# Expert order found on chip by token counts, 64 slots for the four least loaded experts, a ring of nine weight slots

## The chip, the cores and the metric

One core of one Trainium2 chip runs the whole program in one launch. The metric is the device time in microseconds of one execution. Engines are named as in the profile: PE (TensorE matmul), PEld (its weight loads), DVE (VectorE), ACT (ScalarE), POOL (GpSimd), SP (SyncE, which here only issues DMAs and waits). A "q" behind an engine is its instruction queue: "SPq" rows are DMA issues.

## The reference, cut to what matters

Two layers on 256 tokens of 1024 features, all in float32. Layer 0 is dilated attention with a dense SwiGLU, layer 1 is a bidirectional RWKV-7 mixer with a mixture of eight experts, two for each token. The change is in the expert part:

```python
D_MODEL = 1024; SEQ = 256; N_EXPERTS = 8; TOP_K = 2; D_FF_EXPERT = 3584

def swiglu(h, w13, w2):
    gate, up = jnp.split(h @ w13, 2, axis=-1)
    return (jax.nn.silu(gate) * up) @ w2

def moe_swiglu(h, router, w13, w2):
    t = h.reshape(B * S, D)
    logits = (t @ router).astype(jnp.float32)
    top_val, top_idx = lax.top_k(logits, TOP_K)
    gate = jax.nn.softmax(top_val, axis=-1)
    combine = jnp.einsum('tk,tke->te', gate, jax.nn.one_hot(top_idx, N_EXPERTS, dtype=jnp.float32))
    out = jnp.zeros_like(t)
    for e in range(N_EXPERTS):
        out = out + combine[:, e:e + 1].astype(t.dtype) * swiglu(t, w13[e], w2[e])
    return out.reshape(B, S, D)
```

256 tokens with two experts each are 512 rows, 64 for an expert on average. For the inputs drawn with seed 0 the reference's router gives the eight experts 68, 57, 63, 68, 74, 65, 60 and 57 tokens.

## The kernel before, in words

The weights of one expert are 44 MB in 21 units of 2 MB (`U_EXPERT`): 14 "up" units (256 gate and 256 up columns each) and 7 "down" units. `expert_plan` (L129) gives their order: up 0 to 3, down 0, up 4, up 5, down 1, and so on, with downs 5 and 6 at the end. SP moves each unit as two DMAs of 1 MB (`halves`, issued at L597) into a ring of `R = 6` slots of 16 KB per partition. A slot is filled again when PE has used its unit: `wait_free_e` waits for `up_ps` or `down_ps`. Both up units of a pair count as used only after the pair's third run (below).

Experts run in the order 0 to 7, each with room for `CAP = 96` tokens. Tokens that don't fit would be computed in overflow passes after expert 7 (at most 5); each pass loads an expert's 21 units again.

PE's `expert` (L1559) computes for each pair of up units three runs of matmuls: for each unit one with 64 tokens as weights in each half of the array's columns (L1589), then one for both units with the 32 tokens 64 to 95, in four quarters (L1597). A down unit has a run for 64 tokens (L1564, `down_halves`) and one for 32 (L1571, `down_quarters`). ACT takes the SiLU (L2033), DVE multiplies (L2824) and turns the rows for the down product (L2805, L2815).

The router's results are worked on by DVE: ranks (L2724 and on), `choose` for expert 0, `addresses`, `two_rows` (the rows to which each token is copied), `shares` and `overflow_list` (L2749), in this order, and then its part of expert 0. POOL copies the tokens to `xg` in HBM with four indirect DMAs (L3081) once the rows are known. SP loads the tokens of expert n+1 into `xe` behind unit 10 of expert n (L765), and DVE turns them (`next_picked`, L2785). ACT stores each expert's result to `yd` in HBM. After expert 6 POOL gathers each token's rows of results from `yd` into `ya` (L3087), and DVE adds them during expert 7 (L2883). The last expert's result is scattered by PE (L1633, L1637), copied by ACT (L2060) and stored.

The ring's first expert units are issued at the end of the RWKV stage (`for u in range(BWO0, BWO0 + R)`): the two units of `bwo`, then a wait for `head_done` (the last head is normalized), then four expert units, then two more as `bwo`'s slots come free.

Of the kernel before, what the change touches and what calls it, by code (L numbers as in the profile page):

```python
# [6 lines left out]

# [8 lines left out]
F32 = mybir.dt.float32  # L16
I32 = mybir.dt.int32
# [5 lines left out]
P = 128  # L23
# [45 lines left out]
RING_SHIFT = tuple(len(range(r, U_QKV, RQ_SLOTS)) - U_QKV // R if r < RQ_SLOTS else -(U_QKV // R) for r in range(R))  # L69
GE = FFE // 256  # L70
CAP = 96
OVER = 5
# [9 lines left out]
C_ALL = C_CEN + 4 * P  # L82
# [3 lines left out]
def constants():  # L86
# [24 lines left out]
    for n, m in enumerate([(r <= q) - first, (r < q) - first, (r >= q) - last, (r > q) - last]):  # L111
        c[:, C_CEN + n * P:C_CEN + (n + 1) * P] = m
    return c, mask
# [27 lines left out]
def build(nc, x_in, xp_in, pos_in, const_in, mask_in, vec_in, rows_in, qk_rows, qk_cols, wqkv, awo, wrkv, w0, w1, w2, a0, a1, a2,  # L141
          g1, g2, bwo, fw13, fw2, router, mw13, mw2, out):
    ctx = ExitStack()
    with ctx:
# [86 lines left out]
        ones = m.take(P)  # L231
        full_e = m.take(4, 2 * EXPERTS)
# [10 lines left out]
        ya = m.take(2, T, D)  # L243
# [3 lines left out]
        base_e = m.take(EXPERTS)  # L247
# [6 lines left out]
        from_rows = m.take(2, T).bitcast(U32)  # L254

# [66 lines left out]
        E2Tm = [m.take(4, P) for _ in range(2)]  # L322
        Rp = [m.take(2, P) for _ in range(2)]
        m = Region(after_pads + 6 * KB * S, after_pads + 6 * KB * S + 5 * KB * LORA + KB * LORA)
        par_g, rowsB = [], []
        for _ in range(2):
            par_g.append(m.take(RQ))
            rowsB.append(m.take(2, RQ))
        z0e = [m.take(4, RH) for _ in range(2)]
# [16 lines left out]
        ar_late = [[lent.take(2, 2, P) for _ in range(2)] for _ in range(2)]  # L346
        bk = [lent.take(2, 2, P) for _ in range(4)]
        mo_early = [lent.take(4, P) for _ in range(2)]
        mo_first = [lent.take(4, P) for _ in range(2)]
        Xs = lent.take(16, P)  # L350
        lent = Region(5 * SLOT, R * SLOT)
        mo_late = [mo_first, [lent.take(4, P) for _ in range(2)]]
# [27 lines left out]
        slot_full = [sem(f"slot_full{i}") for i in range(R)]  # L380
# [14 lines left out]
        lg_ps, lg_sb, lg_ex = (sem(n) for n in ("lg_ps", "lg_sb", "lg_ex"))  # L395
        chosen_ok, place_ps, total_ps, over_ok = (sem(n) for n in ("chosen_ok", "place_ps", "total_ps", "over_ok"))
# [7 lines left out]
        gate_ps, gn_ms, gn_rt, db_ready = (sem(n) for n in ("gate_ps", "gn_ms", "gn_rt", "db_ready"))  # L404
# [31 lines left out]
        xg = nc.dram_tensor("xg", (EXPERTS * CAP + 2 * S, D), F32).ap()  # L436
        yd = nc.dram_tensor("yd", ((EXPERTS - 1) * CAP + 1, D), F32).ap()
# [85 lines left out]
        plans = [expert_plan(MOE0), expert_plan(MOE0 + U_EXPERT)]  # L523

        def arrived(eng, u, rounds=0):

            nth = u // RQ_SLOTS if u < U_QKV else u // R + RING_SHIFT[u % R]
            eng.wait_ge(slot_full[slot_of(u)], rounds * 32 + (nth + 1) * 32)

        def slot_of(u):  # L530

            return u % RQ_SLOTS if u < U_QKV else u % R
# [19 lines left out]
        free_e = {}  # L552
        for e in range(2):
            for kind, n, u in plans[e]:
                free_e[u] = (up_ps, e * UPS + 3 * (n // 2) + 3) if kind == "up" else (down_ps, e * GE // 2 + n + 1)
        per_turn = {up_ps: 2 * UPS, down_ps: GE}

        def wait_free_e(sp, u, i):

            w = u - R  # L560
            if w < MOE0 and isinstance(i, int) and i == 0:
                s, n = free[w]
                sp.wait_ge(s, n)
                return
            back = 0
            if w < MOE0:
                w, back = w + 2 * U_EXPERT, 1
            s, n = free_e[w]
            for t, per in per_turn.items():
                if s is t:  # L570
                    sp.wait_ge(s, i * per + (n - back * per))


        over_plan = expert_plan(U_QKV)
        over_uses = [len([v for v in range(U_EXPERT) if v % R == r]) for r in range(R)]
        uses = [len([u for u in range(MOE0 + EXPERTS * U_EXPERT) if u % R == r]) + RING_SHIFT[r] for r in range(R)]

# [15 lines left out]
        def _(sp):  # L593
# [80 lines left out]
            def rest_unit(u):  # L674
                if u < MOE0:
                    square(u, bwo[:, (u - BWO0) * 512:(u - BWO0 + 1) * 512])
                else:
                    expert_unit(plan_e[u - MOE0], 0)

            plan_e = [(e, *a) for e in range(2) for a in plans[e]]  # L680

            def expert_unit(item, i):

                e, kind, n, u = item
                tiled_unit(u, (mw13 if kind == "up" else mw2)[bass.ds(i * 2 + e, 1), n])
# [46 lines left out]
            key_rows(1)  # L732
            gate_params(0)
            gate_params(1)
            sp.wait_ge(za.ps, 2)
            lora_params(1)
# [17 lines left out]
            for u in range(BWO0, BWO0 + R):  # L754
                if u == BWO0 + U_BWO:
                    sp.wait_ge(head_done, NQ + 1)
                wait_free(u)
                rest_unit(u)

            def next_rows(item, i):  # L760

                e, at = item[0], plans[item[0]].index(item[1:])
                if at == 10 and not (isinstance(i, int) and i * 2 + e == EXPERTS - 1):
                    sp.wait_ge(picked_sb, (i * 2 + e + 1) * 2)
                    sp.dma_start(xe[0:CAP], xg[bass.ds((i * 2 + e + 1) * CAP, CAP), :]).then_inc(xe_in, 16)  # L765

            first = BWO0 + R - MOE0
            assert first < 10
            for item in plan_e[first:]:
                wait_free_e(sp, item[3], 0)  # L770
                expert_unit(item, 0)
                if item[3] == plans[0][9][2]:
                    sp.wait_ge(xg_in, 64)
                next_rows(item, 0)
            for i in range(1, EXPERTS // 2 - 1):
                for item in plan_e:
                    wait_free_e(sp, item[3], i)
                    expert_unit(item, i)
                    next_rows(item, i)
            for item in plan_e:  # L780
                wait_free_e(sp, item[3], EXPERTS // 2 - 1)
                expert_unit(item, EXPERTS // 2 - 1)
                next_rows(item, EXPERTS // 2 - 1)

            sp.wait_ge(over_ok, 1)
            many = sp.value_load(over_i[0:1, 0:1], min_val=0, max_val=OVER)
            with sp.Fori(0, OVER) as j:
                with sp.If(j < many):
# [4 lines left out]
                    for kind, n, u in over_plan:  # L793
                        if u >= U_QKV + R:
                            s, c = freed[u - U_QKV - R]
                            per = UPS if s is up_ps else GE // 2
                            sp.wait_ge(s, j * per + (EXPERTS * per + c))
                        tiled_unit(u, (mw13 if kind == "up" else mw2)[bass.ds(e, 1), n])
# [7 lines left out]
        def _(pe):  # L806
# [727 lines left out]
            run(ps[:, 6, 0:EXPERTS], [(ones, chosen[:, 0, :]), (ones, chosen[:, 1, :])]).then_inc(total_ps, 1)  # L1534
# [16 lines left out]
            def scatter(n, b, back, width):  # L1551

                pe.wait_ge(y_sb, n * 2 + 4)
# [5 lines left out]
            def expert(n, c, b, plan, landed, before_last=None):  # L1559
# [16 lines left out]
                for kind, g, u in plan:  # L1576
# [3 lines left out]
                    if kind == "up":  # L1580
                        w = unit(u).rearrange("p (k n) -> p k n", n=512)
                        p = g // 2
                        if p >= 2:
                            pe.wait_ge(hide_sb, n * UPS + (3 * (p - 2) + g % 2 + 1))
# [1543 lines left out]
```

## Time and profile before

| | |
|---|---|
| median of 3 runs | 1832.61 us (1832.45 to 1833.87) |
| span of the profiled execution | 1837.4 us |
| PE busy in it | 1787.1 us (97%) |
| DVE, ACT, POOL busy | 948.7, 349.1, 235.8 us |
| moved by DMA | 473.62 MB, of it 336 transfers of 1 MB from `mw`, the experts' weights |
| chain that ended last | PE 91%, DVE 5%, ACT 2%, DMA 1% |

The profiled execution took 4.8 us (0.3%) more than the median of the runs. In the page, part 2 cuts the span into 40 slices of 45.9 us, where each digit is a busy share in tenths; the experts fill the slices from the 21st on. A busy engine in this profile need not be the only limit: DMA engines and PE can both be full.

### The profile page before, as it was taken

To read this page: it belongs to the slowest core of one execution; us is meant where nothing else is said; L and a number is where in the kernel's file an instruction comes from. 1 tells how busy PE (TensorE), PEld (TensorE's weight loads), DVE (VectorE), ACT (ScalarE), POOL (GpSimd) and SP (SyncE) were. 2 spreads that over 40 slices of the span, in tenths; PEclk is the share of its full clock that TensorE was granted. 3 is DMA by queue.
4 is the path that set the end of the run, shared out by engine and by line. 5 is a ranking of instruction groups with operands and counts; after the bars stand their busy time and mean duration, and the time that the engine had idled before them with its cause. 6 is when DMAs were issued, how large, how long until landed. Compare 5 with 4: busy or idle time off the path is not lost.

```text
span 1837.4 us, 36427 instructions
## 1 busy us (share of the span) xinstructions
PE 1787.1 (97%) x15674; PEld 1173.0 (64%) x15674; DVE 948.7 (52%) x2350; ACT 349.1 (19%) x747; POOL 235.8 (13%) x319
## 2 busy tenths in 40 slices
PE   8999999999999998898999999999999999999998
PEld 5888885788445587887665555555555555555554
DVE  6667653655574567754364345354444544435442
ACT  3234332122012253352110000000000000000001
POOL 2432320100011434433000000000000000000000
PEclk9999999999999999999989999999999999999999
DMA  8552436744631011012479999999999999999994
GB/s 310 184 183 90 140 120 205 247 155 167 200 137 41 6 25 33 11 19 99 172 284 406 396 401 418 401 399 409 409 410 389 417 409 393 418 400 416 403 421 168
DMA packets 137958, 473.62 MB, mean 258 GB/s; under 512 B 30168, under 2 KB 59120, under 8 KB 94784
## 3 DMA queue, kind: packets, MB, share of 16 engines
q1 hardware_dynamic: 133904, 459.82, 64.9%
q0 software_dynamic: 2080, 7.37, 1.2%
q10 hardware_dynamic: 1808, 4.03, 0.6%
q8 instruction: 126, 2.06, 0.5%
q14 instruction: 40, 0.33, 0.1%
HBM read 461.09 MB, written 10.10 MB: 256 GB/s over the span
## 4 chain that ended last, share of the span: by engine, by line
PE 91%; DVE 5%; ACT 2%; DMA 1%; issue 1%; SPq 0%; POOL 0%; DVEq 0%
PE ps L1589 21%; PE ps L812 12%; PE ps L994 11%; PE ps L1597 11%; PE ps L1564 11%; PE ps L866 10%; PE ps L1571 5%; PE ps L1162 2%; PE ps L858 1%; PE ps L1008 1%; PE ps L1523 1%; PE ps L1509 1%; PE ps L886 1%; PE ps L820 1%; DVE arena L2530 1%
## 5 line engine op out<-in xcount | busy, mean ns | idle before, releaser
L1589 PE MATMUL ps<-arena 128*64 128x256 f32 x3584 | 397.1, 380 | 0.0
L1589 PEld LDWEIGHTS ps<-arena 128*64 128x64 f32 x3584 | 256.0, 137 | 150.3 <-issue 29.0
L812 PE MATMUL ps<-arena 128*128 128x128 f32 (+9 forms) x1946 | 279.5, 320 | 20.6 <-DVE arena L2518 9.1
L2824 DVE TENSOR_TENSOR arena<-arena,ps 64x256 f32<-64x256 f32 x168 | 71.3, 425 | 403.7 <-ACT arena L2033 403.6
L812 PEld LDWEIGHTS ps<-arena 128*128 128x128 f32 (+3 forms) x1946 | 222.2, 187 | 73.6 <-issue 39.3
L994 PE MATMUL ps<-arena 128*128 128x256 f32 x952 | 210.7, 379 | 0.1
L1597 PE MATMUL ps<-arena 128*32 128x256 f32 x3584 | 205.0, 381 | 0.0
L2033 ACT ACTIVATE arena<-ps 64x256 f32<-64x256 f32 x168 | 63.2, 376 | 738.9 <-PE ps L1589 554.3
L1564 PE MATMUL ps<-arena 128*64 128x512 f32 x896 | 203.1, 598 | 0.0
L994 PEld LDWEIGHTS ps<-arena 128*128 128x128 f32 x952 | 178.6, 190 | 23.8 <-issue 0.5
L866 PE MATMUL ps<-arena 128*128 128x256 f32 (+1 forms) x714 | 189.1, 425 | 0.0
L1597 PEld LDWEIGHTS ps<-arena 128*32 128x32 f32 x3584 | 111.0, 110 | 88.6 <-issue 21.5
L866 PEld LDWEIGHTS ps<-arena 128*128 128x128 f32 x714 | 134.8, 190 | 50.6 <-issue 34.4
L2805 DVE STREAM_TRANSPOSE arena<-arena 32x128 f32<-32x128 f32 x448 | 136.4, 304 | 7.3
L1564 PEld LDWEIGHTS ps<-arena 128*64 128x64 f32 x896 | 60.0, 136 | 119.9 <-issue 119.9
L2815 DVE STREAM_TRANSPOSE arena<-arena 32x64 f32<-32x64 f32 x448 | 106.5, 238 | 7.3
L1571 PE MATMUL ps<-arena 128*32 128x256 f32 x1792 | 107.2, 379 | 0.0
L3087 POOL DMA_INDIRECT arena<-yd,arena x4 | 3.8, 955 | 779.2 <-DMA yd<-arena 778.3
L2282 DVE TENSOR_TENSOR arena<-arena 128x1024 f32<-128x1024 f32 (+3 forms) x92 | 86.0, 959 | 22.0 <-PE ps L866 20.9
L1571 PEld LDWEIGHTS ps<-arena 128*32 128x32 f32 x1792 | 57.6, 110 | 43.4 <-issue 6.5
L1933 ACT ACTIVATE arena<-ps 128x512 f32<-128x512 f32 (+1 forms) x80 | 43.8, 560 | 49.5 <-PE ps L812 41.6
L2785 DVE STREAM_TRANSPOSE arena<-arena 32x128 f32<-32x128 f32 x168 | 50.9, 303 | 2.5
(304 smaller groups left out, 1440.0 us busy)
## 6 DMA issues: line engine op xcount, KB each, us to landing
arena<-mw SPq DMA_DIRECT2D x336, 1024.0 KB, 12.0
arena<-wqkv SPq DMA_DIRECT2D x35, 1024.0 KB, 7.3
arena<-fw SPq DMA_DIRECT2D x32, 1024.0 KB, 7.5
arena<-wrkv SPq DMA_DIRECT2D x12, 1024.0 KB, 7.3
arena<-awo SPq DMA_DIRECT2D x4, 1024.0 KB, 6.4
arena<-bwo SPq DMA_DIRECT2D x4, 1024.0 KB, 8.6
xg<-arena POOLq DMA_DIRECT2D x8, 384.0 KB, 9.0
arena<-xg SPq DMA_DIRECT2D x7, 384.0 KB, 17.1
```

Source lines behind the costliest of these rows:

```text
L812: last = mm(o, a, b, start=(n == 0), stop=(n == len(pairs) - 1))
L866: last = mm(ps[:, bank, 0:b.shape[2]], a[:, k, :], b[:, k, :], start=(start and k == 0), stop=(stop and k == n - 1), skip_group_check=True)
L994: last = mm(ps[:, bank, 0:256], a[:, k, :], b[:, k, :], start=(start and k == 0), stop=(stop and k == 3), skip_group_check=True)
L1564: last = mm(ps[r, 5, :], hidT[:, g % 2, k, 0:64], w[:, k, a * 512:(a + 1) * 512], start=(first and k == 0), stop=(end and k == 3), skip_gr ...
L1571: last = mm(ps[r, 6, 0:256], hidT[:, g % 2, k, 64:CAP], w[:, k, a * 256:(a + 1) * 256], start=(first and k == 0), stop=(end and k == 3), s ...
L1589: last = mm(ps[r, g % 4, 0:256], picked[:, b, k, 0:64], w[:, k, a * 256:(a + 1) * 256], start=(k == 0), stop=(k == KB - 1))
L1597: last = mm(ps[r, (7, 4)[p % 2], 0:256], picked[:, b, k, 64:CAP], pair[a % 2][:, k, a // 2 * 256:a // 2 * 256 + 256], start=(k == 0), stop ...
L2033: act.activation(sg_e[RH:P, j % 2, :], ps[0:RH, bank, 0:256], ACT.Silu).then_inc(sge_sb, 1)
L2282: dve.tensor_tensor(out, a, b, op).then_inc(sums_ok, 1)
L2805: dve.transpose(o[:, :, :, 32 * i:32 * i + 32], src[:, :, :, j, :])
L2815: last = dve.transpose(o[:, a, :, 64:CAP], src[:, :, j, :])
L2824: dve.tensor_tensor(hid_e[RH:P, p % 2, j % 3, :], sg_e[RH:P, j % 2, :], ps[RH:P, bank, 0:256], ALU.mult).then_inc(hide_sb, 1)
```

## The change

1. Order. From the token counts (PE's sums in `ps` bank 6) DVE's new function `turns` ranks the experts by count on chip, with expert 0 always first (`C_FORCE`), and gives turn n the rank `RANK_AT[n]` = 0, 4, 1, 5, 2, 6, 3, 7. Turns 1, 3, 5 and 7 thus take the four least loaded experts, if expert 0 is among the other four or not. SP reads each turn's expert number from `expert_no` and loads from that address. Places, weights and rows are put in turn order (`in_turn`). `turns` stands ahead of `addresses`; `overflow_list` moves from there to turn 1, behind DVE's pair 5 (`aside`).
2. Room. The light turns have `LIGHT = 64` slots and `per = 2` runs for each pair: the runs for tokens 64 to 95 (L1597, L1571) and their SiLU, product and turning are left out, each up unit's slot is free after its own run, and `xe`, `xg` and `yd` have 64 rows for them. Up to `OVER = 6` overflow passes.
3. Ring. Nine slots for the experts' units, in the order 3, 4, 5, 0, 6, 8, 1, 2, 7 (eight in the last turn: slot 8 is then `ya`). Small buffers of the RWKV stage move so that they fit. `first_free` lets the first nine units start as their slots' earlier use ends, the first right behind `bwo`; only the sixth still waits for `head_done`.
4. `gate_params(0)` and `(1)` are issued behind `lora_params(1)` and a wait for `rkv_ps` 8. Some semaphores are merged.

```diff
-OVER = 5
+OVER = 6
+LIGHT = 64
+RANK_AT = (0, 4, 1, 5, 2, 6, 3, 7)
+IS_LIGHT = tuple(r >= 4 for r in RANK_AT)
+ROOM = tuple(LIGHT if a else CAP for a in IS_LIGHT)
+RUNS_AT = tuple((2 if a else 3) * (GE // 2) for a in IS_LIGHT)
...
+        in_line = collections.deque((3, 4, 5, 0, 6, 8, 1, 2, 7))
+        for u in range(MOE0, MOE_END):
+            if u == MOE_END - U_EXPERT:
+                in_line.remove(8)
+            slot_in_turn.append(in_line[0])
+            in_line.rotate(-1)
...
-            gate_params(0)
-            gate_params(1)
             sp.wait_ge(za.ps, 2)
             lora_params(1)
+            sp.wait_ge(rkv_ps, 8)
+            gate_params(0)
+            gate_params(1)
             diagonal_blocks(0)
...
+            def first_free(u):
+                slot = slot_of(u)
+                if slot == 4:
+                    sp.wait_ge(E.ps, chain(NQ - 1, 1, 1))
+                elif slot in (5, 0, 6):
+                    sp.wait_ge(Y.ps, NQ)
+                elif slot == 8:
                     sp.wait_ge(head_done, NQ + 1)
+                elif slot in (1, 2):
+                    sp.wait_ge(*free[before_it[u]])
+                elif slot == 7:
+                    sp.wait_ge(lg_ps, T)
+            e = 0
+            for u in range(MOE0, MOE_END):
+                n, at = (u - MOE0) // U_EXPERT, (u - MOE0) % U_EXPERT
+                if n and at == 0:
+                    sp.wait_ge(order_ok, 1)
+                    e = sp.value_load(expert_no[0:1, n:n + 1], min_val=0, max_val=EXPERTS - 1)
+                if u < MOE0 + R + 3:
+                    first_free(u)
+                else:
+                    sp.wait_ge(*free[before_it[u]])
+                expert_unit(u, e)
+                if at == 10 and n + 1 < EXPERTS:
                     sp.wait_ge(xg_in, 64)
+                    sp.wait_ge(picked_sb, (n + 1) * 2)
+                    sp.dma_start(xe[0:ROOM[n + 1]], xg[ROWS0[n + 1]:ROWS0[n + 2], :]).then_inc(xe_in, 16)
...
+            def in_turn(dst, src):
+                n = src.shape[1]
+                link(dve.tensor_tensor(cmp_a[:, 0:n], turn_of.unsqueeze(1).broadcast_to([P, n, EXPERTS, EXPERTS]),
+                                       src.unsqueeze(2).broadcast_to([P, n, EXPERTS, EXPERTS]), ALU.mult))
+                link(dve.tensor_reduce(dst, cmp_a[:, 0:n], AX, ALU.add))
+            def turns():
+                E = EXPERTS
+                dve.wait_ge(place_ps, 2)
+                link(dve.tensor_copy(counts, ps[:, 6, 0:E]))
+                link(dve.tensor_tensor(keyed, counts, const[:, C_FORCE:C_FORCE + E], ALU.max))
+                other, own = keyed.unsqueeze(1).broadcast_to([P, E, E]), keyed.unsqueeze(2).broadcast_to([P, E, E])
+                link(dve.tensor_tensor(cmp_a[:, 0], other, own, ALU.is_gt))
+                link(dve.tensor_tensor(cmp_b[:, 0], other, own, ALU.is_equal))
+                link(dve.tensor_tensor(cmp_b[:, 0], cmp_b[:, 0], tie, ALU.mult))
+                link(dve.tensor_tensor(cmp_a[:, 0], cmp_a[:, 0], cmp_b[:, 0], ALU.add))
+                link(dve.tensor_reduce(rank, cmp_a[:, 0], AX, ALU.add))
+                link(dve.tensor_tensor(turn_of, ..., ALU.is_equal))
+                in_turn(expert_at[:, 0:1], const[:, C_ROW:C_ROW + E].unsqueeze(1))
+                dve.tensor_copy(expert_no, expert_at[:, 0]).then_inc(order_ok, 1)
+                in_turn(place2[:, :, 0:E], p8)
+                link(dve.tensor_copy(p8, place2[:, :, 0:E]))
+                in_turn(comb[:, :, 1:E + 1], logits)
+                link(dve.tensor_copy(comb[:, :, E + 1:2 * E + 1], comb[:, :, 1:E + 1]))
...
-                        if g % 2:
+                        if g % 2 and not light:
                             ...
                             for k in range(KB):
                                 for a, r in enumerate(QUADS):
                                     last = mm(ps[r, (7, 4)[p % 2], 0:256], picked[:, b, k, 64:CAP], ...)
...
+                        if light:
+                            down_halves(g, w, first, end).then_inc(down_ps, 1)
...
             picked_out(1, 0, CAP)
+            turns()
             addresses()
...
-            overflow_list()
...
+            for n in range(EXPERTS - 1):
+                expert(n, RUNS0[n], IS_LIGHT[n], n * 16 + 16, None, (n + 1) % 2, overflow_list if n == 1 else None)
```

## Rows read from the trace of the kernel before

**Rows 1.** The page, part 2: GB/s moved by DMA in 40 slices.

```profile
GB/s 310 184 183 90 140 120 205 247 155 167 200 137 41 6 25 33 11 19 99 172 284 406 396 401 418 401 399 409 409 410 389 417 409 393 418 400 416 403 421 168
```

**Rows 2.** Timeline of one period: start us, us, engine, line, count.

```profile
1201.05 7.08 PE L1589 MATMUL ps<-arena 128*64 128x256 f32 x64
...
1208.06 3.66 PE L1597 MATMUL ps<-arena 128*32 128x256 f32 x64
...
1211.54 1.91 PE L1571 MATMUL ps<-arena 128*32 128x256 f32 x32
...
1213.38 3.65 PE L1564 MATMUL ps<-arena 128*64 128x512 f32 x16
...
1216.86 7.08 PE L1589 MATMUL ps<-arena 128*64 128x256 f32 x64
```

**Rows 3.** SP's waits, 936 to 1811 us: total us, times, longest.

```profile
SPq L597 <- PE ps L1597: 534.0, 55, 26.0
```

**Rows 4.** DMA from 947.5 to 1810.5 us: busy tenths in 40 slices, total.

```profile
DMA  9999999999999999999999999999999999999998
...
DMA packets 49068, 349.33 MB, mean 405 GB/s; under 512 B 5504, under 2 KB 5504, under 8 KB 7503
```

**Rows 5.** Stretches: us, busy PE, PEld, DVE, ACT, POOL, clock, DMA share, GB/s.

```profile
932.00:947.50 15.50, 15.50 (x155) 11.23 (x154) 9.57 (x51) 0.96 (x3) 4.02 (x4) 0.86 0.25 99
...
1000.00:1100.00 100.00, 100.00 (x1132) 54.76 (x1132) 41.83 (x139) 8.34 (x21) 0.00 (x0) 1.00 1.00 400
...
1182.00:1212.00 30.00, 30.00 (x332) 16.57 (x332) 9.88 (x34) 2.10 (x6) 0.00 (x0) 1.00 0.99 375
1212.00:1260.00 48.00, 48.00 (x544) 26.41 (x540) 25.61 (x84) 3.55 (x10) 0.00 (x0) 1.00 1.01 419
```

**Rows 6.** DMA from 1800 to 1838 us in 40 slices of 0.95 us.

```profile
GB/s 423 423 431 431 397 414 345 190 43 52 0 0 0 0 0 0 0 0 0 0 0 17 0 0 0 0 0 9 0 0 9 17 0 177 367 272 276 30 9 0
```

**Rows 7.** The chain that ended last, its last pieces: start us, us, what.

```profile
1819.58 3.58 PE ps L1564 x16
1823.16 1.86 PE ps L1571 x32
1825.03 3.63 PE ps L1633 x8
```

**Rows 8.** Timeline of PE, POOL and DVE around the first expert's start.

```profile
936.83 7.13 PE L1589 MATMUL ps<-arena 128*64 128x256 f32 x64
...
941.76 1.11 POOL L3081 DMA_INDIRECT xg<-arena  x1 [16.20 <-DVE arena L2866]
...
944.72 0.23 DVE L2754 TENSOR_TENSOR arena<-arena 128x64 f32<-128x64 f32 x1
...
950.42 0.18 DVE L2765 CAST arena<-arena 128x11 int32<-128x11 f32 x1
...
954.43 2.00 DVE L2815 STREAM_TRANSPOSE arena<-arena 32x64 f32<-32x64 f32 x8
...
958.02 1.91 PE L1571 MATMUL ps<-arena 128*32 128x256 f32 x32
```

**Rows 9.** Timeline of SP's queue, 540 to 980 us.

```profile
573.68 0.49 SPq L700 DMA_DIRECT2D arena<-g  x1
...
623.41 3.77 SPq L710 DMA_DIRECT2D xd<-arena  x8
...
850.15 2.21 SPq L597 DMA_DIRECT2D arena<-bwo  x4
897.80 66.60 SPq L597 DMA_DIRECT2D arena<-mw  x22
```

**Rows 10.** Timeline of ACT: the copy behind the eighth `rkv_ps`.

```profile
608.82 0.60 ACT L1856 ACTIVATE arena<-ps 128x512 f32<-128x512 f32 x1 [6.53 <-PE ps L812]
```

**Rows 11.** Stretches ahead of a fall of the clock, columns as in rows 5.

```profile
840.80:847.60 6.80, 4.61 (x92) 3.72 (x90) 6.60 (x12) 0.54 (x2) 6.00 (x11) 1.00 0.09 25
847.60:851.00 3.40, 1.41 (x42) 1.14 (x37) 0.53 (x1) 0.61 (x2) 3.17 (x4) 1.00 0.32 34
```

More of the change, by code:

```diff
@@ L8 @@
+import collections
 import math
@@ L68 @@
 U_EXPERT = 21
-RING_SHIFT = tuple(len(range(r, U_QKV, RQ_SLOTS)) - U_QKV // R if r < RQ_SLOTS else -(U_QKV // R) for r in range(R))
 GE = FFE // 256
 CAP = 96
-OVER = 5
+OVER = 6
[4 more added lines that the diff above has]
+RUNS_AT = tuple((2 if a else 3) * (GE // 2) for a in IS_LIGHT)
+RUNS0 = tuple(sum(RUNS_AT[:n]) for n in range(EXPERTS + 1))
+RESULTS0 = tuple(2 + sum(1 if a else 2 for a in IS_LIGHT[:n]) for n in range(EXPERTS + 1))
+ROWS0 = tuple(sum(ROOM[:n]) for n in range(EXPERTS + 1))
+FULL = EXPERTS
 C_ID = 0
@@ L231, in build @@
         ones = m.take(P)
+        counts = m.take(EXPERTS)
+        keyed = m.take(EXPERTS)
+        rank = m.take(EXPERTS)
+        turn_of = m.take(EXPERTS, EXPERTS)
+        expert_at = m.take(2, EXPERTS)
+        expert_no = m.take(EXPERTS).bitcast(I32)
         full_e = m.take(4, 2 * EXPERTS)
@@ L328, in build @@
             rowsB.append(m.take(2, RQ))
+        m = Region(after_pads + 6 * KB * S, after_pads + 6 * KB * S + 5 * KB * LORA + KB * LORA)
+        assert m.at <= LATE_AT
+        E2Tm = [m.take(4, P) for _ in range(2)]
+        Rp = [m.take(2, P) for _ in range(2)]
         z0e = [m.take(4, RH) for _ in range(2)]
@@ L377, in mo_of @@
             return mo_late[q % 2][i // 2] if i % 2 else mo_early[i // 2]
-        slot_full = [sem(f"slot_full{i}") for i in range(R)]
+        slot_full = [sem(f"slot_full{i}") for i in range(R + 3)]
         in_x = [sem("in_x0"), sem("in_x1")]
@@ L548, in down_quarter @@
             return unit(DN0 + j)[:, 0:2 * h * D].rearrange("p (k n) -> p k n", n=D)[:, h * i:h * i + h, 512 * n:512 * n + 512]
[L552 to L576, printed above, removed]
+        for n, plan in enumerate(plans):
+            for kind, g, u in plan:
+                if kind == "down":
+                    free[u] = (down_ps, n * (GE // 2) + g + 1)
+                elif IS_LIGHT[n]:
+                    free[u] = (up_ps, RUNS0[n] + g + 1)
+                else:
+                    free[u] = (up_ps, RUNS0[n] + 3 * (g // 2) + 3)
+        over_plan = expert_plan(MOE_END)
+        over_uses = [slot_in_turn[MOE_END:].count(r) for r in range(R)]
         def x_scale(t):
@@ L672, in _, with expert_unit @@
                 square(RKV0 + n, wrkv[n // 2, :, (n % 2) * 512:(n % 2 + 1) * 512])
[L674 to L685, printed above, removed]
+            def expert_unit(u, e):
+                kind, g, _ = plans[(u - MOE0) // U_EXPERT][(u - MOE0) % U_EXPERT]
+                tiled_unit(u, (mw13 if kind == "up" else mw2)[bass.ds(e, 1), g])
             def tiled_unit(u, w):
@@ L1557, in scatter, with expert @@
                     run(ps[:, (4, 7, 0, 1)[k], :], [(pickT[0:width, b, t, :], yb[0:width, h * 512:(h + 1) * 512])]).then_inc(back_ps, 1)
-            def expert(n, c, b, plan, landed, before_last=None):
+            def expert(n, runs, results, light, c, b, plan, landed, before_last=None):
+                per = 2 if light else 3
                 def down_halves(g, w, first, end):
@@ L2782, in next_picked @@
                 rows = xe[:, 512 * half:512 * half + 512].rearrange("p (k j f) -> p k j f", j=4, f=32)
-                for i in range(CAP // 32):
+                for i in range(room // 32):
                     for j in range(4):
```

281 lines of the change are left out of this document (139 added, 142 removed).

## The prediction

> **What bounds the kernel now.** I read the slices of the page first. From the 22nd slice to the 39th DMA moves 389 to 421 GB/s and never rests; this is the expert stage, and nowhere else are two slices in a row above 300 [rows 1]. The change is about PE's work in this stage, so the question is which of PE and DMA sets its length. The timeline of PE shows a strict period of 1216.86 - 1201.05 = 15.81 us for each pair of up units and its down unit, without a wait: 7.01 us for the two runs of 64 tokens, 3.48 for the quarters with tokens 64 to 95, 1.84 for the down quarters and 3.48 for the down halves, each taken from start to start [rows 2]. Seven periods are 110.7 us for an expert and 885.4 for eight. SP waits 534 us for L1597 to free slots [rows 3], so PE sets the pace. But the view of DMA over the same stage shows that nothing is left there either: 349.33 MB in 863 us, 405 GB/s, with every slice but the last at nine tenths or more [rows 4]. The cleanest stretch, without a token load or a result store, has 419 GB/s at a DMA share of 1.01; a stretch with the load of `xe` has 375, and the first full 100 us have 400 [rows 5]. A PE period takes three units, 6.29 MB, so PE asks for 398 GB/s of weights alone. PE and DMA are full at once, and only what shortens both shortens the stage.
>
> **Part 1, PE's runs.** A light expert loses 3.48 + 1.84 = 5.32 us of 15.81 in each of seven periods [rows 2]: 37.2 us, and four of them 149 us. A light expert alone would then ask for 6.29 MB in 10.49 us, 600 GB/s. No row has this. A heavy and a light turn together are 110.7 + 73.4 = 184.1 us of PE, but 42 units, 88.1 MB, which at 405 GB/s take 217 us. Nine slots let PE run ahead for part of the first light turn; after that it waits for weights. I count these 149 us as nothing by themselves: PE will wait for DMA instead. The end is then set by the DMA stream: its start, its bytes, its rate, and the work behind its last unit.
>
> **Part 2, the start of the stream.** Before, four expert units are issued from 897.80 on, behind `head_done`, and two more when `bwo` frees its slots [rows 9]; then DMA falls to 99 GB/s between 932 and 947.5, a share of 0.25, since all six slots are full [rows 5]. The seventh unit starts when PE has freed the first pair: 936.83 + 10.49 + about 0.2 = 947.5 [rows 8, 2]. After, nine units fit. The first can be issued right behind `bwo` at 852 [rows 9], at a time when the page has 99 to 172 GB/s [rows 1], and all nine should land by about 938. PE's first turn is heavy in both kernels and needs the same runs, so the stream restarts at 947.5 again, but three units, 6.29 MB, are behind it already.
>
> **Part 3, the bytes of the stream.** 349.33 MB of before [rows 4], less 6.29 for the three units, less 0.52 for the four light loads of `xe` (128 KB less each), less 0.39 for three light stores of `yd`, plus 1.5 for the scatter to `xg`: in before it mostly ran in the idle 932 to 947.5 (99 GB/s for 15.5 us) and now it comes later (next part). That is 343.6 MB. At 405 GB/s it takes 848 us. The load of `xe` costs more than its bytes: 30 us at 375 instead of 419 lose 3.2 us for 0.39 MB, which alone would take 0.9 [rows 5]. Four loads that are a third smaller save about one us each instead of 0.3, so I take 845 us. Bounds: at 419 GB/s throughout 820 us, at the 400 of the slowest 100 us 859 [rows 5].
>
> **Part 4, DVE's `turns`.** About 17 small instructions. DVE's like ones between 944.72 and 950.42 follow each other at about 0.2 to 0.3 us [rows 8], so 17 x 0.27 = 4.6 us, between 2 (if it were only 0.12 each) and 8. It stands ahead of `addresses`; queued behind it on DVE are the row numbers, for which POOL's scatter waits, and the products of the first pair. `overflow_list`, 944.5 to 950.6, leaves this place, so DVE reaches its first expert about 1.5 us earlier than before. That matters as PE's first down at 958.02 has only 1.6 us over the end of DVE's turning at 956.43 [rows 8]. Cost nothing; should `turns` take 8 us, PE would lose 0.3. The scatter starts at 946.4 instead of 941.76, hence its bytes in the sum. SP waits for it ahead of the first `xe` load, now near 948; behind that wait is unit 11, whose slot is free only at 958, so nothing is late. `overflow_list` in turn 1, now some 46 instructions or 10 us, delays DVE's pair 6 there; PE could wait some 3 us for it in front of the last down, at a time when it is ahead of what DMA allows. Nothing. If DMA were no limit, 3 us.
>
> **Part 5, SP.** The address of a turn's expert comes from a register. SP waits for `order_ok` (about 941) at unit 21, which is issued near 1000, and nothing is late. Issues with a register address are not in the trace; a 1 MB issue takes SP some 0.43 us, and with six or more units queued in front of DMA even 2 us more would be hidden. A deeper queue is not in the trace of this stage either; I take no change and leave its risk to the range. The moved `gate_params` wait for the eighth `rkv_ps`, which ACT's copy shows at 608.82 [rows 10]. Behind the wait stands `diagonal_blocks(0)`, whose first DMA is at 623.41, so four issues of about 0.5 us fit in between [rows 9]. First use of the gates is after that. Nothing; without this cover it would cost these 2 us. The next `xe` lands behind unit 10, while PE still waits for units 11 and 12; DVE's block there has a period of DMA as cover.
>
> **Part 6, the end.** Before, the weights stop at about 1809.5 [rows 6], while PE starts the last unit only at 1819.58 [rows 7]: it is ten us behind the stream. After, PE stands at the end waiting for the last unit. Behind it come 3.58 us of halves (the 1.86 of quarters are gone), and then what lies between 1825.03 and the end of the span at 1837.4, 12.4 us [rows 7]: 16.0.
>
> **The sum.** 947.5 + 845 + 16.0 = 1808.5 us of span. The profiled span was 4.8 us above the median of the runs, so 1803.7; I say 1803. PE's own time would be 936.8 + 4 x 184.1 + 12.4 = 1685.6; the difference of 123 us should show as waits of PE for `mw`.
>
> [...]
>
> **Rivals.** (a) PE alone decides and DMA follows at any rate. For it: PE has no wait in the stage, and SP waits for PE. Against it: the DMA share of 1.00 at 400 to 419 GB/s. Time 1685.6 - 4.8 = 1681. Chance 0.03.
> (b) The stream is faster than its mean once the stage holds fewer loads, stores and PE reads: 420 GB/s or above, 818 us, and 947.5 + 818 + 16.0 - 4.8 = 1777. For it: the slices at 421 [rows 1]. Against: the dips come with token loads, which stay. Chance 0.12.
> (c) The clock, on the slower side. [...] Chance 0.05. [...]
> (d) A deeper queue or register addresses slow the stream to 390 GB/s: 881 us, 1840. No row has such a queue beside full-speed PE. Chance 0.10 for anything from 1818 up, about half of it below 1829.
> (e) The change doesn't save what it says, as an expert has more tokens than room: an overflow pass loads 44 MB more, 109 us, and about 20 us around it, 1932. The reference's counts give the heavy turns 68, 74, 68, 65 and the light turns 63, 60, 57, 57, all within room. Chance 0.02.
>
> **How the numbers follow.** The forecast, a stage bound by DMA at the rate of before, has 0.68 and its own range is 1786 to 1818 (the rates 400 to 415). About 0.2% is what a measurement of this kernel can tell from no change, so the same is 1829 to 1836. Faster: 0.68 + 0.03 + 0.12 + half of (d) = 0.88. Same 0.04. Slower 0.08: the rest of (d), (c) and (e). The range reaches from the 419 GB/s bound, 1779, up to 1824, half way into (d).
>
> **What would show each step.** Right: DMA share 1.0 and 400 to 419 GB/s from 947.5 to about 1793; no slice at 99 GB/s apart from the few us before 947.5; the first `mw` issue near 852; PE waiting some 120 us for DMA `mw`, nearly all in light turns; 64-token periods of 10.5 us where PE has weights; L1597 and L1571 with half of their counts; the first expert matmul within one us of 936.8; the last unit's run within 1 us of its landing. Wrong: PE waits well below 100 us with an early end would be (b) or (a); clock marks below 1.0 in light turns would be (c); mean rate below 400 with share 1.0 would be (d).

## The result and the profile after

The changed kernel takes 1803.76 us (median of 4 runs, 1802.29 to 1806.16) against 1832.6: a ratio of 0.9833, 95% interval 0.9815 to 0.9851, 28.8 us less. Forecast were 1803 and a range of 1779 to 1824.

The page of the changed kernel: span, part 2 with PE, clock, DMA and GB/s in 40 slices of 45.0 us, and the chain that ended last.

```profile
span 1800.6 us, 31353 instructions
...
PE   8999999999999998998999997999779996799877
...
PEclk9999999999999999999989999999999999999999
DMA  9452426754640000102759999999999999999995
GB/s 328 176 187 80 155 97 204 234 179 170 180 182 24 24 22 13 31 17 79 285 198 387 419 398 420 419 400 419 394 421 409 403 420 389 421 401 413 419 421 244
...
SPq L623 27%; PE ps L837 12%; PE ps L1019 11%; PE ps L891 10%; DMA arena<-mw 6%; PE ps L1616 6%; PE ps L1624 3%; PE ps L1591 3%; PE ps L1187 2%; PE ps L883 1%; PE ps L1598 1%; PE ps L1548 1%; PE ps L1534 1%; PE ps L1033 1%; PE ps L911 1%
```

PE now has sevens and sixes where it had nines, while DMA has nines as before and moves 387 to 421 GB/s, the level of [rows 1]. In the expert stage the chain no longer runs mainly through the experts' matmuls (before, L1589, L1597 and L1564 had 43% of the span) but through SP's issues (L623, 27%) and the landing of `mw` (6%). The three following views are of the stage alone. First, what PE waits for from 930 us on (in all, times, longest, us):

```profile
PE ps L1616 <- DMA arena<-mw: 64.2, 47, 2.7
PE ps L1591 <- DMA arena<-mw: 38.7, 25, 3.5
```

Second, DMA from 945 to 1782 us, busy tenths and total, the answer to [rows 4]:

```profile
DMA  8999999999999999999999999999999999999998
...
DMA packets 48078, 341.70 MB, mean 408 GB/s; under 512 B 5417, under 2 KB 5417, under 8 KB 7433
```

Third, the timeline of the first expert's start and the end of the chain, the answers to [rows 8] and [rows 7]:

```profile
929.63 7.13 PE L1616 MATMUL ps<-arena 128*64 128x256 f32 x64
...
940.40 2.05 SPq L623 DMA_DIRECT2D arena<-mw  x4
...
958.32 0.45 SPq L806 DMA_DIRECT2D arena<-xg  x1
```

```profile
1757.10 27.14 DMA arena<-mw
1784.24 0.04 issue
1784.28 3.65 PE ps L1591 x16
1787.94 3.63 PE ps L1660 x8
```

The stream restarts 10.8 us behind the first expert matmul and its last transfer lands at 1784.2, 843.8 us later. PE starts the last down unit 0.04 us behind it, where before it was ten us late [rows 6, 7].

The part ahead of the experts is of different length in different executions of the same code (last section), so the profiles are compared by the time from the first expert matmul to the end of the span, called the stage below. It is 1837.4 - 936.8 = 900.6 us before and 1800.6 - 929.6 = 871.0 after, 29.6 less, near the 28.8 of the medians. (A span is 1.7 us shorter than the time of the same execution: 1800.6 against 1802.29.)

### The profile page after: what moved, and what is told of

Read it like the earlier page. It is cut to its first block, busy times and chain, and to the rows that moved or that the text cites. A ratio compares the mean times of both kernels' runs of the same rounds, so it can differ in the third digit from the quotient of the medians.

```text
span 1800.6 us, 31353 instructions
## 1 busy us (share of the span) xinstructions
PE 1650.3 (92%) x12986; PEld 1082.1 (60%) x12986; DVE 873.5 (49%) x2082; ACT 339.2 (19%) x719; POOL 236.2 (13%) x319
## 4 chain that ended last, share of the span: by engine, by line
PE 56%; SPq 28%; DMA 7%; DVE 5%; ACT 2%; issue 2%; POOL 0%; DVEq 0%
SPq L623 27%; PE ps L837 12%; PE ps L1019 11%; PE ps L891 10%; DMA arena<-mw 6%; PE ps L1616 6%; PE ps L1624 3%; PE ps L1591 3%; PE ps L1187 2%; PE ps L883 1%; PE ps L1598 1%; PE ps L1548 1%; PE ps L1534 1%; PE ps L1033 1%; PE ps L911 1%
## 5 line engine op out<-in xcount | busy, mean ns | idle before, releaser
L1616 PE MATMUL ps<-arena 128*64 128x256 f32 x3584 | 405.2, 382 | 64.2 <-DMA arena<-mw 64.2
L2884 DVE TENSOR_TENSOR arena<-arena,ps 64x256 f32<-64x256 f32 x140 | 59.5, 426 | 473.5 <-ACT arena L2061 473.4
L1591 PE MATMUL ps<-arena 128*64 128x512 f32 x896 | 207.0, 606 | 38.7 <-DMA arena<-mw 38.7
L2061 ACT ACTIVATE arena<-ps 64x256 f32<-64x256 f32 x140 | 52.8, 377 | 723.0 <-PE ps L1616 631.0
L1591 PEld LDWEIGHTS ps<-arena 128*64 128x64 f32 x896 | 60.6, 138 | 162.4 <-issue 110.8
L2862 DVE STREAM_TRANSPOSE arena<-arena 32x128 f32<-32x128 f32 x448 | 136.3, 304 | 7.3
L1624 PE MATMUL ps<-arena 128*32 128x256 f32 x1792 | 102.5, 380 | 0.0
L1624 PEld LDWEIGHTS ps<-arena 128*32 128x32 f32 x1792 | 55.0, 110 | 44.8 <-issue 10.8
L2873 DVE STREAM_TRANSPOSE arena<-arena 32x64 f32<-32x64 f32 x224 | 53.3, 238 | 3.6
L1598 PE MATMUL ps<-arena 128*32 128x256 f32 x896 | 53.6, 379 | 0.0
L2842 DVE STREAM_TRANSPOSE arena<-arena 32x128 f32<-32x128 f32 x136 | 41.2, 303 | 5.1 <-DMA arena<-xg 3.0
L1598 PEld LDWEIGHTS ps<-arena 128*32 128x32 f32 x896 | 28.4, 110 | 22.1 <-issue 3.2
## 6 DMA issues: line engine op xcount, KB each, us to landing
arena<-mw SPq DMA_DIRECT2D x336, 1024.0 KB, 26.9
```

What stands on the lines that cost most here:

```text
L1591: last = mm(ps[r, 5, :], hidT[:, g % 2, k, 0:64], w[:, k, a * 512:(a + 1) * 512], start=(first and k == 0), stop=(end and k == 3), skip_gr ...
L1598: last = mm(ps[r, 6, 0:256], hidT[:, g % 2, k, 64:CAP], w[:, k, a * 256:(a + 1) * 256], start=(first and k == 0), stop=(end and k == 3), s ...
L1616: last = mm(ps[r, g % 4, 0:256], picked[:, b, k, 0:64], w[:, k, a * 256:(a + 1) * 256], start=(k == 0), stop=(k == KB - 1))
L1624: last = mm(ps[r, (7, 4)[p % 2], 0:256], picked[:, b, k, 64:CAP], pair[a % 2][:, k, a // 2 * 256:a // 2 * 256 + 256], start=(k == 0), stop ...
L2862: last = dve.transpose(o[:, :, :, 32 * i:32 * i + 32], src[:, :, :, j, :])
L2873: last = dve.transpose(o[:, a, :, 64:CAP], src[:, :, j, :])
```

## The experiments

All are edits of the changed kernel, unless named otherwise. Ratios are to the kernel before on the same chip. The experiments ran on four chips, where the kernel before has medians of 1834.2 to 1838.2 us against the 1832.6 of the result, so a difference between two ratios of up to some 0.003 (5 us) need not be the edit's. Where a step is that small, the stage in the profile decides, and it is one execution.

| run | edit | ratio (95%) | stage, us |
|---|---|---|---|
| changed | | 0.9833 (0.9815 to 0.9851) | 871.0 |
| e1 | all turns 96 slots | 0.9996 (0.9985 to 1.0008) | 902.1 |
| e2 | six ring slots | 0.9883 (0.9861 to 0.9904) | 884.0 |
| e3 | all turns 64 slots | 0.9753 (0.9734 to 0.9771) | 858.5 |
| e4 | a quarter fewer bytes | 0.9169 (0.9151 to 0.9188) | 751.0 |
| e5 | before, a quarter fewer bytes | 1.0005 (0.9995 to 1.0015) | 900.5 |
| e6 | first wait for the scatter later | 0.9812 (0.9799 to 0.9825) | 866.7 |
| e7 | no loads of `xe` | 0.9711 (0.9696 to 0.9726) | 848.8 |
| e8 | 96-slot turns first | 0.9787 (0.9769 to 0.9806) | 873.2 |
| e9 | `xe` loaded to 128 partitions | 0.9757 (0.9743 to 0.9771) | 857.2 |
| e10 | e6 and e9 | 0.9734 (0.9716 to 0.9752) | 854.7 |
| e11 | first units start as before | 0.9819 (0.9802 to 0.9836) | 870.1 |
| e12 | e10 and e8 | 0.9795 (0.9778 to 0.9812) | 863.7 |

**e1: everything but the light turns.**

```diff
-IS_LIGHT = tuple(r >= 4 for r in RANK_AT)
+IS_LIGHT = tuple(False for r in RANK_AT)
```

> The changed kernel, but every turn has 96 slots and three runs for each pair; order on chip, nine ring slots and the early start stay. Theory 'both full' (before, PE and DMA were both full; without fewer PE runs PE sets the stage again): eight heavy experts of 110.7 us behind the same first matmul, so 1832 us, ratio to before 0.998 to 1.001, and no waits of PE for mw. Rival 'ring' (the gain of 29 us comes from nine slots and the early start alone): 1804 to 1818 us.

Measured 0.9996. PE has no wait for `mw` and its period is the old one, as the timeline of PE shows:

```profile
1205.39 3.66 PE L1624 MATMUL ps<-arena 128*32 128x256 f32 x64
1208.87 1.91 PE L1598 MATMUL ps<-arena 128*32 128x256 f32 x32
1210.71 3.65 PE L1591 MATMUL ps<-arena 128*64 128x512 f32 x16
1214.19 6.00 PE L1616 MATMUL ps<-arena 128*64 128x256 f32 x54
```

Ring, early start, `turns` and the moved `gate_params` together neither gain nor cost anything that can be measured. Without fewer PE runs a faster stream is worth nothing.

**e2: the light turns without the ring.** `in_line` is (3, 4, 5, 0, 1, 2) and `first_free` waits for `head_done` at slot 3.

> The changed kernel with the light turns, but the ring has six slots in the old order and its first expert unit waits for the last head as before. Theory 'stream': the same bytes less nothing, and the three units that were behind the stream's restart come back into it, 6.29 MB at 405 GB/s = 15.5 us: 1819 us (1816 to 1824). Rival 'ring': all the gain goes, 1832 us. Rival 'PE': the light turns' runs alone carry the gain, so it stays at 1804 us.

Measured 0.9883, 0.005 or 9 us above the changed kernel, and 13.0 us in the profiled stage: the last unit lands 13.7 us later after the first expert matmul (868.3 instead of 854.6). "Stream" is confirmed, its 15.5 us a little too high. Of the 29 us 17 to 21 come with the light turns on six slots and 9 to 13 with the three more.

**e3: no 96-slot turn at all.** `IS_LIGHT` is all true, and the overflow list stays empty.

> The changed kernel with 64 slots and two runs in all eight turns and no overflow pass: tokens beyond an expert's 64th are left out. PE has 149 us less to do than in the changed kernel. Theory 'stream': the weights are the same bytes, only three loads of xe and four stores of yd are 128 KB smaller (0.9 MB, 2 to 4 us), so 1798 to 1803 us. Rival 'PE': 1655 us. If PE's work counts in part (the heavy turns, where both are full), something between, 1770 to 1790 us.

Measured 0.9753: PE has 149 us less to do and the kernel is 15 us faster (12.5 in the stage), so PE's work is not the limit. But I expected 2 to 4 us. The trace shows where the larger part comes from: in a light turn 0 PE frees the first slot after one run, and the stream restarts 4 us after the first matmul instead of 10.8. That is 7 of the 12.5, the smaller loads and stores 2 (0.9 MB). The other 3 to 4 us lie at the loads of `xe`: by the packets of the two traces, and against 420 GB/s, the last six loads lose 12.7 us of stream beyond their bytes here and 16.7 in the changed kernel. Why they lose less here was not followed.

**e4 and e5: a quarter fewer bytes, after and before.**

```diff
-                halves(u, (unit(u)[:, 0:half], unit(u)[:, half:]), (w[:, 0:half], w[:, half:]))
+                end = SLOT if u < MOE0 + 9 else SLOT - half // 2
+                halves(u, (unit(u)[:, 0:half], unit(u)[:, half:end]), (w[:, 0:half], w[:, half:end]))
```

> The changed kernel, but from the tenth expert unit on each unit's second half is loaded to one half only, so a unit moves 1.57 MB instead of 2.10; PE's work is unchanged (the rest of the slot holds old weights). The stream is 83 MB or 205 us shorter, less than PE's work. Theory 'stream': PE sets the stage, 4 x 184.1 us of it, 1681 us (1678 to 1690), and its waits for mw nearly vanish. Rival: if PE's waits come from SP's queue (register addresses, more waits) and not from the rate of DMA, they stay and the time is above 1740 us.

> The kernel before, with the same cut as in e4: from the tenth expert unit on a unit moves 1.57 MB instead of 2.10, PE's work unchanged. Theory 'both full': PE alone already set the pace before, with DMA just able to follow, so 1832 us on the first chip, ratio 0.998 to 1.001. Rival: if DMA had been the slower one there, each 1% of bytes would show, and the time falls by 20 us or more.

Measured 0.9169, 1680 us on the scale of the first chip, and 1.0005. With bytes to spare (371 GB/s at a DMA share of 0.94 in the first line below, columns as in [rows 5]) the changed kernel runs at the rate of its PE work, and PE waits 3.1 us in all from 950 to 1680:

```profile
1200.00:1300.00 100.00, 100.00 (x900) 54.67 (x897) 42.23 (x133) 8.35 (x21) 0.00 (x0) 1.00 0.94 371
...
PE ps L1592 <- DVE arena L2863: 3.1, 3, 2.8
```

The same cut brings nothing before. This pair carries the main reading: before, PE set the pace and DMA could just follow; after, DMA sets it, and 751.0 against 871.0 us of stage is what the light turns would be worth to PE alone.

**e6: SP's first wait for the scatter later.** From the trace of the changed kernel: SP issues units 9 and 10 at 940.4, then waits for the scatter to `xg` until 958.3, although PE has freed the slots of units 11 and 12 at 950.8. The windows of that time (us, busy of PE, PEld, DVE, ACT, POOL, clock, DMA share, GB/s) show DMA at rest for about half of 955 to 960:

```profile
945.00:955.00 10.00, 10.00 (x132) 5.23 (x129) 7.64 (x28) 0.75 (x2) 0.00 (x0) 1.00 1.00 413
955.00:960.00 5.00, 5.00 (x44) 2.83 (x40) 0.00 (x0) 0.18 (x1) 0.00 (x0) 1.00 0.46 167
960.00:966.00 6.00, 6.00 (x85) 3.54 (x84) 2.64 (x8) 0.57 (x2) 0.00 (x0) 1.00 1.01 390
```

```diff
-                if at == 10 and n + 1 < EXPERTS:
+                if at == (10 if n else 12) and n + 1 < EXPERTS:
```

> The changed kernel, with one edit: in turn 0 SP issues the first load of xe behind unit 12 instead of unit 10, so that units 11 and 12 do not stand behind SP's wait for the scatter (in the trace of the changed kernel that wait ends at 958.3, the slots of units 11 and 12 are free at 950.8, and DMA falls to 35 GB/s at 958 to 960). Theory 'stream': the stream is never interrupted again, 3.5 us less, 0.9814 of before. Rival: turn 0 is set by PE and the ring is refilled anyway, so the gap costs nothing and the ratio stays 0.9833.

Measured 0.9812, 0.0021 less, as "stream" wanted, but the intervals of the two ratios overlap, so the times don't settle it. The profiled stage is 4.3 us shorter and its last unit lands 3.7 us earlier after the first expert matmul, with the stream restarting 10.8 us behind that matmul in both. I take the gap as worth about 4 us, on this one pair of profiles.

**e7: the loads of `xe` taken out** (turns 1 to 7 compute on a constant).

> The changed kernel without the seven loads of xe (turns 1 to 7 compute on a constant instead of their tokens; SP's waits stay). Seven loads are 2.2 MB of 342. Theory 'bytes': 5.5 us less than the changed kernel, 0.980 of before. Theory 'slow packets' (while a load's 4 KB packets are in the queue, the weights' 8 KB packets take some 550 ns instead of 313, which loses about 2.5 us for each load beside its bytes): 20 to 24 us less, 0.970 to 0.972 of before.

Measured 0.9711, 22 us less than the changed kernel (22.2 in the stage): a load costs 3.2 us on average, while its 0.26 to 0.39 MB would be 0.6 to 0.9. "Slow packets" is right. A load in the changed kernel, in windows with the columns above:

```profile
1054.00:1066.00 12.00, 12.00 (x92) 6.50 (x90) 3.81 (x12) 1.13 (x3) 0.00 (x0) 1.00 1.02 423
1066.00:1072.00 6.00, 6.00 (x48) 3.26 (x46) 2.34 (x8) 0.08 (x1) 0.00 (x0) 1.00 1.03 259
```

The DMA share is full in both, the rate falls by two fifths. In the trace the weights' packets of 8 KB have a median of 313 ns in the first window and 506 ns in the second, where one in ten takes over 630. The stores of `yd`, from 96 or 64 partitions as well, do no such harm: they are still there in e7, and DMA keeps 417 to 423 GB/s in every slice of its stage but the first and the last.

**e9: the same loads to all 128 partitions.**

```diff
-                    sp.dma_start(xe[0:ROOM[n + 1]], xg[ROWS0[n + 1]:ROWS0[n + 2], :]).then_inc(xe_in, 16)
+                    sp.dma_start(xe[0:P], xg[ROWS0[n + 1]:ROWS0[n + 1] + P, :]).then_inc(xe_in, 16)
```

> The changed kernel, but each load of xe takes 128 rows to all 128 partitions instead of 96 or 64 (the rows beyond are not used; 1.4 MB more in all, 3.5 us at the stream's rate). Theory 'spread': the weights' packets slow down because a load to 96 or 64 partitions is laid out over the DMA engines in another way than the weights are; with 128 partitions this goes, 17 us less for the slow packets and 3.5 more for the bytes, 13 us less than the changed kernel, 0.976 of before. Rival 'rows': it is the 4 KB rows or where xg lies in HBM, so there are more of them now and the kernel is 3 to 9 us slower than the changed one, 0.985 to 0.988 of before.

Measured 0.9757, 0.0076 or 14 us less than the changed kernel, with more bytes. DMA from 945 to 1782 us in 40 slices:

```profile
GB/s 338 420 419 420 419 422 417 420 422 419 418 420 420 418 420 421 419 420 422 419 420 419 419 419 420 420 421 421 420 422 418 420 420 419 421 419 420 421 419 182
```

Every dip is gone but the first. So it was neither the 4 KB rows, of which there are more now, nor their place in HBM, but how many partitions (or rows, the two go together here) a load has. Why that is so no view here shows: the traces don't tell which DMA engine writes which partitions. That such a load is laid out over the DMA engines in another way than the weights, as "spread" has it, stays a guess of mine: the time and the dips agree with it, and no run tests the layout itself.

**e10: e6 and e9 together.**

> e9 and e6 together: loads of xe to 128 partitions, and SP's first wait for the scatter behind unit 12. Theory 'stream': both shorten the same stream at different places, so they add up: 0.9757 - 0.0021 = 0.9736 of before. Rival: with the stream faster, the heavy turns are set by PE (110.7 us against 21 units at 4.97 and a load of 1.2, 105.6), DMA rests there, and the second gain is lost: 0.9757.

Measured 0.9734, or 1784 us on the scale of the first chip: the fastest kernel of this study that leaves nothing out, 49 us below the kernel before and 18 below the change. DMA from 945 to 1765 us:

```profile
GB/s 400 419 418 420 417 421 419 420 421 421 418 420 420 419 420 420 422 421 420 422 419 416 420 419 420 422 419 421 420 419 422 419 419 420 419 420 418 421 420 360
```

By the ratios the gains add up (0.0076 and 0.0021 against 0.0099). By the stages the second is 2.5 us, but e10's stream restarts 13.6 us behind the first expert matmul and e9's 10.8.

**e11: nine slots, late start.** `first_free` waits for `head_done` at slot 3 too.

> The changed kernel with nine slots, but the first expert unit waits for the last head as in the kernel before (the early issue behind bwo goes). Theory 'slots': nine units at 5.0 us from 890 on are in by about 936, before PE has freed the first pair, so only the number of slots counts and the time stays, 0.982 to 0.985 of before. Rival 'early start': the early issue carries the 13 us between the six-slot and the nine-slot kernel, 0.988.

Measured 0.9819 and within 1 us the same stage as the changed kernel. The number of slots counts; that the first units start 43 us earlier does not, as far as this can tell. The equal stages hide two differences of about 4 us each. In e11 the granted clock was 0.5 of full speed until 934.0, 3.6 us into the experts' matmuls (in the changed kernel until 929.4, 0.2 us ahead of them), and the stream restarts 15.2 us behind the first of them instead of 10.8; but the scatter had landed by 948.2, within 9 us of its first issue, and the gap of e6 is not there.

**e8 and e12: the order of the turns.**

```diff
-RANK_AT = (0, 4, 1, 5, 2, 6, 3, 7)
+RANK_AT = (0, 1, 2, 3, 4, 5, 6, 7)
```

> The changed kernel with the turns in order of count, the four with 96 slots first and the four with 64 last (RANK_AT 0 to 7). Theory 'stream': DMA is full in every turn, so the order moves nothing: the same bytes, within 4 us of the changed kernel, 0.981 to 0.986 of before; PE's waits all lie in the last four turns. Rival 'interleave' (every second turn must be light, so that PE's lead from one is used in the next): four heavy turns in a row are set by PE at 110.7 us and fall behind, some 10 us or more slower than the changed kernel, 0.989 or above.

> e10 with the order of e8 (the four turns with 96 slots first). E8 measured 0.9787 where the changed kernel had 0.9833, though its profile from the first expert matmul to the end is 2.3 us longer. Theory 'stream' (the order moves nothing, E8's ratio is the spread of the part ahead of the experts): 0.973, within 0.002 of e10, and 854 to 858 us from the first expert matmul to the end. Rival 'order' (light turns last are worth 8 us): 0.969, and 847 us or less there.

E8 measured 0.9787, faster than the changed kernel and outside what both theories expected, while its profiled stage is 2.3 us longer. That profile is of the slowest of its four executions (1806.3 us, median 1799.9), and it has the late restart of e11 (15.2 us) and no gap. E12 was made to decide this, and it measured 0.9795 where e10 has 0.9734: 11 us slower, and 9.0 in the stage. Both expectations of e12 fell; what I had called "interleave" for e8 is what happened. Two windows of e12, one in its 96-slot turns and one in its 64-slot turns, and the first of them for e10:

```profile
1200.00:1300.00 100.00, 100.00 (x1102) 54.55 (x1100) 44.08 (x145) 8.34 (x21) 0.00 (x0) 1.00 1.00 408
...
1500.00:1600.00 100.00, 71.74 (x524) 35.53 (x520) 26.23 (x81) 5.70 (x14) 0.00 (x0) 1.00 1.01 421
```

```profile
1200.00:1300.00 100.00, 86.86 (x768) 45.69 (x764) 31.85 (x100) 7.20 (x18) 0.00 (x0) 0.97 1.01 420
```

With the loads mended DMA can deliver 21 units in 105 us (an estimate: 44.0 MB at the 420 GB/s of e10), and a heavy turn takes PE 110.7. Four of them in a row are set by PE again, at 404 to 419 GB/s, and the light turns behind them can't win the time back. With every second turn light, PE has the lead of one turn to use in the next. While the loads cost 3 us each, as in the change (3.2 by e7), a heavy turn takes DMA nearly as long as PE, by the same estimate some 108 us against 110.7, and the order moves the stage little: 2.3 us in these profiles. That e8's ratio is 8 us below the changed kernel's stays open: its profile does not show it, and e12 speaks against a gain from the order. Part of it can be the chip: e11, nearly the changed kernel and measured on e8's chip, is only 3.8 us above e8, and their intervals just overlap.

## Why the prediction was right, point by point

**What bounds it.** That PE and DMA were both full before, and that 149 us less of PE's work would only turn DMA into the bound, is shown by e1, e4, e5 and, with e3, from the other side.

**The stream.** Forecast 845 us from its restart to the last landing, measured 843.8. The bytes were forecast at 343.6 MB and are 343.32 from 940.4 to 1784.3, the mean rate 405 against 407 GB/s. Single terms were less exact. A load of `xe` was read off as 3.2 us from 375 against 419 GB/s [rows 5], and four light ones as one us less each: some 18 us for seven, where e7 measured 22. The light loads save only their bytes: beyond them, by the packets of the trace against 420 GB/s, those of 64 rows lose 2.3, 3.0 and 2.9 us and those of 96 rows 2.3, 2.9 and 3.3 (the seventh load falls into the gap of e6). The three units ahead, taken at 15.5 us, were worth 9 to 13 (e2).

**`turns` and the scatter.** DVE's `turns` runs from 930.2 to 934.4, 4.2 us where 4.6 were forecast, and DVE starts its part of turn 0 at 941.3, 11.7 us behind the first expert matmul instead of 13.8, earlier as said. The step "nothing is late" failed. I let the scatter land 9 us after its first issue, as before, and let unit 11 wait for its slot until then. It took from 938.8 to 958.3, 19.5 us, and the slot was free at 950.8. It now shares DMA with two units of weights: e6 has 19.5 us again, and in e11, where the restart comes later, it lands within 9. The missed term is about 4 us (e6). It did not show in the total because the stretches without a load ran at about 420 GB/s, more than the mean of before that the sum goes by.

**SP, register addresses, the deeper queue.** A transfer now takes 26.9 us from issue to landing in the median, against 12.0 before, with the rate unchanged at 417 to 424 GB/s in slices without a load. Rival (d) fell. `gate_params` went out at 606.1, ahead of `xd` at 620.7, as forecast.

**The end.** 16.0 us forecast from the last landing to the end, 1800.6 - 1784.2 = 16.4 measured.

**PE's waits.** 102.9 us of waits for `mw`, where "some 120" was said, and 92 of them in light turns. That number was the difference between span and PE's own time, which is 1800.6 - (929.6 + 736.4 + 12.4) = 122.2 now. The 19 us between are in no wait of the view. Some 5 of them are matmuls at half clock, an estimate from the three stretches below and the 1.7 us that a run lost over one of them. Another 13 are an estimate from the timelines: a run that the next follows takes 3.48 us from start to start and one followed by a wait 3.66, and PE waits 72 times.

**The clock.** Rival (c), the clock on the slower side, had 0.05. No run shows light turns whose length the clock sets. What they show in its place: in light turns of the changed kernel the granted clock falls from 1.00 to 0.50 of full speed three times, for 3.4 us each. Two of them, in windows of the changed kernel:

```profile
1284.50:1291.30 6.80, 3.27 (x28) 1.67 (x26) 2.86 (x9) 0.38 (x1) 0.00 (x0) 1.00 1.02 292
1291.30:1294.70 3.40, 3.40 (x12) 0.97 (x10) 2.69 (x9) 0.00 (x0) 0.00 (x0) 0.50 0.98 402
...
1694.10:1700.90 6.80, 4.52 (x38) 2.49 (x36) 2.75 (x9) 0.38 (x1) 2.37 (x3) 1.00 1.00 414
1700.90:1704.30 3.40, 3.40 (x12) 0.97 (x9) 0.11 (x1) 0.00 (x0) 0.00 (x0) 0.50 1.02 419
```

Ahead of the first, a load of `xe` had slowed the stream to 292 GB/s, PE was busy 3.27 of 6.80 us, and the granted clock fell to 0.50. Ahead of the second no load of `xe` was under way; PE was busy 4.52 of 6.80 us, about the 4.61 of the first line of [rows 11], behind which the clock stayed at 1.00 for another 3.40 us. In both stretches at 0.50 PE was busy all the time, and behind them the clock was 1.00 again. The down run (L1591) that lay over either of them took 5.35 us instead of 3.65, 1.7 more. The stream went on at 402 and 419 GB/s meanwhile, so nothing was lost. In e3, where PE is busy 71 to 75 us of each 100, seven such stretches of 3.4 and two of 6.8 us left DMA at 410 to 418 GB/s as well. What it would have taken to be slower than before is an estimate: four pairs of turns are 736 us at full speed, all light work in twice its time, as over those two stretches, would add 294, and the kernel before is reached at 888, with about 52% of the light work at half clock.

**What was luck.** The profiled span of before was 4.8 us above the median time, that of after is 3.2 below it. I forecast a span of 1808.5 and got 1800.6; 7.2 of these 7.9 us lie ahead of the first expert matmul (936.8 against 929.6), a point at which I had said "within one us". The medians don't have this difference, and taking off the 4.8 put the forecast on their scale. That the medians met within 1 us is in part luck: the stage was forecast at 1808.5 - 936.8 = 871.7 us and took 871.0, but with 4 us too little for the scatter and 3 us taken off for light loads that hardly save anything, made up by the faster stream between the loads.

## What to carry to other kernels

Before you cut the work of the engine on the critical path, look at the DMA share and rate of the same stretch: where both are full, the cut is worth only what the other resource has left, and here 149 us of PE bought 29, of which 9 to 13 needed three more ring slots. In a DMA-bound stage count the time from the restart of the stream, bytes at the measured rate, and the work behind the last landing; then look for what slows the packets (a small load to 64 or 96 partitions cost in the mean about four times what its bytes take) and for waits in the queue that issues them. Once the stream runs at its full rate, put turns with less compute between turns with more, so that no stretch is set by the other engine (e12 against e10, 9 to 11 us).

## What the runs showed of the hardware that was not expected

A load to 96 partitions beside a full stream of loads to 128 takes the whole of DMA from 423 to 259 GB/s for some 6 us at a full DMA share, one to 64 partitions to 297 GB/s for 7 us (1174 to 1181 us in the changed kernel); the same rows in a load to 128 partitions leave it at 417 to 422 in every slice of the stage but the first and the last (e9), and so do stores from 96 or 64 partitions (e7).

The part ahead of the experts varies between executions of the same code. The first expert matmul starts at 929.6 to 931.3 us in the profiles of the changed kernel, e2, e7, e8, e10 and e11, and at 933.1 to 936.1 in e1, e3, e4, e6, e9 and e12; 934.8 and 936.8 in the two executions of before. In each of the first group the clock falls once between 560 and 860 us, for 3.4 us; in each of the second, and before, it falls two or three times there, for 3.4 or 6.8 us. A profiled span should not be compared with another to better than 7 us here without looking at where the parts begin.

The stream ends unevenly. In its last 12 us, 1771.6 to 1783, the changed kernel's rate sinks step by step from 388 to 164 GB/s, and the busy share of its DMA engines with it, from nine tenths to three (why was not followed). Busy tenths and rate in slices of 0.95 us, from 1763 us on:

```profile
DMA  9999999999887666665531000000000004958000
GB/s 414 423 414 423 423 414 423 423 423 388 354 345 302 267 267 259 259 259 224 207 164 43 9 9 0 0 0 0 0 17 0 0 0 138 384 211 354 26 9 0
```

PE waits for the last of them. By the mean of about 270 GB/s over these 12 us against 420, some 4 us of full rate are lost, an estimate; whether a shorter queue at the end would save them was not tried.
